# A diffusion backbone step: a warm-up, an earlier first product, moved query slices and later weight chunks in the first head

## What is computed

```python
c      = silu(c_ctx), silu(c)                    # two conditioning vectors of 2048
mod    = c @ w_ada + b_ada                       # w_ada 2048 x 6144: shift, scale, gate
h      = rms_norm(x, norm_w) * (1 + scale) + shift
proj   = h @ w_in                                # w_in 2048 x 9216, nine parts of 1024
# parts 0, 1: q, k of retention; 2, 3: its v and gate; 4, 5, 6: q and two forget
# gates of HGRN2; 7, 8: its v and gate; eight heads of 128 in each part
# two scans over chunks, forward and backward, per head and group
out    = concat(o_r, o_h) @ w_out                # 2048 x 2048
y      = rms_norm(x + gate * out) * final_norm_w
```

## Time and profile before

| | |
|---|---|
| median of 3 runs | 1426.14 us (1426.08 to 1426.21) |
| profiled execution | 1426.52 us, span 1424.7 us |
| TensorE busy | 1404.5 us, 99% of the span |
| TensorE loading weights | 1184.8 us, 83% |
| VectorE busy | 970.9 us, 68% |
| ScalarE busy | 496.7 us, 35% |
| GpSimd busy | 367.9 us, 26% |
| HBM read and written | 174.41 and 16.53 MB, 134 GB/s over the span |
| mean granted TensorE clock | 0.998 |

### The profile page before, as it was taken

One profiled execution on the slowest core, in us unless ns is written; L12 is line 12 of the kernel. 1 busy time (PEld: TensorE's weight loads), 2 busy tenths in 40 slices (PEclk: granted clock), 3 DMA queues, 4 the chain that ended last, 5 costly groups with the idle time before them and its releaser, 6 DMA issues.

```text
span 1424.7 us, 24851 instructions
## 1 busy us (share of the span) xinstructions
PE 1404.5 (99%) x10220; PEld 1184.8 (83%) x10220; DVE 970.9 (68%) x1293; ACT 496.7 (35%) x893; POOL 367.9 (26%) x292
## 2 busy tenths in 40 slices
PE   6999999999999999999999999999999999999997
PEld 4788898889888988898889888988898888888886
DVE  4655676666689778977887788766676668632345
ACT  4323243334333433343334333423342334321234
POOL 0000114311432153215321532153114315301220
PEclk9999999999999999999999999999999999999999
DMA  9994222322333333323432333322223347183235
GB/s 387 409 404 169 79 94 83 89 91 73 127 126 109 107 126 124 119 99 126 130 115 97 126 134 111 97 97 88 83 68 97 89 148 256 48 286 112 89 104 206
DMA packets 68870, 196.66 MB, mean 138 GB/s; under 512 B 7824, under 2 KB 16288, under 8 KB 63904
## 3 DMA queue, kind: packets, MB, share of 16 engines
q1 hardware_dynamic: 68736, 195.15, 39.7%
q10 hardware_dynamic: 32, 0.02, 0.0%
HBM read 174.41 MB, written 16.53 MB: 134 GB/s over the span
## 4 chain that ended last, share of the span: by engine, by line
PE 97%; DVE 1%; DMA 1%; ACT 0%; issue 0%; SPq 0%; DVEq 0%; ACTq 0%
PE ps L2013 10%; PE ps L2015 10%; PE ps L2014 10%; PE ps L1846 9%; PE ps L1848 8%; PE ps L1847 8%; PE ps L1822 8%; PE ps L2196 5%; PE ps L2198 5%; PE ps L2197 5%; PE ps L2030 2%; PE ps L1855 2%; PE ps L1853 2%; PE ps L1854 2%; PE ps L1812 2%; PE ps L2041 1%
## 5 line engine op out<-in xcount | busy, mean ns | idle before, releaser
L1139 DVE TENSOR_TENSOR w_lo<-area,w_hi 128x1024 fp32r<-128x1024 f32 x143 | 184.4, 1289 | 253.5 <-ACT w_hi L675 253.5
L675 ACT ACTIVATE w_hi<-area 128x1024 fp32r<-128x1024 f32 x143 | 151.7, 1061 | 500.4 <-PE ps L2015 292.8
L2013 PE MATMUL ps<-w_hi,hT_hi 128*128 128x512 f32 x640 | 252.1, 394 | 0.0
L2015 PE MATMUL ps<-w_hi,hT_lo 128*128 128x512 f32 x640 | 249.4, 390 | 0.0
L2014 PE MATMUL ps<-w_lo,hT_hi 128*128 128x512 f32 x640 | 249.2, 389 | 0.0
L1846 PE MATMUL ps<-hT_hi,w_hi 128*128 128x512 f32 x512 | 205.6, 401 | 0.5 <-DVE hT_lo L1191 0.4
L1847 PE MATMUL ps<-hT_lo,w_hi 128*128 128x512 f32 x512 | 199.7, 390 | 0.0
L1848 PE MATMUL ps<-hT_hi,w_lo 128*128 128x512 f32 x512 | 199.7, 390 | 0.0
L2015 PEld LDWEIGHTS ps<-w_hi,hT_lo 128*128 128x128 f32 x640 | 120.1, 188 | 25.4
L2013 PEld LDWEIGHTS ps<-w_hi,hT_hi 128*128 128x128 f32 x640 | 120.2, 188 | 24.3
L2014 PEld LDWEIGHTS ps<-w_lo,hT_hi 128*128 128x128 f32 x640 | 120.3, 188 | 24.0
(11 more groups left out here) (279 smaller groups left out, 2463.7 us busy)
## 6 DMA issues: line engine op xcount, KB each, us to landing
area<-in_w_in SPq DMA_DIRECT2D x144, 512.0 KB, 3.9
area<-in_w_mod SPq DMA_DIRECT2D x32, 1024.0 KB, 8.8
area<-in_w_out SPq DMA_DIRECT2D x38, 512.0 KB, 3.7
gate_raw<-in_w_gate SPq DMA_DIRECT2D x32, 512.0 KB, 3.7
o_hi_scratch<-area SPq DMA_DIRECT2D x14, 320.0 KB, 2.2
o_lo_scratch<-area SPq DMA_DIRECT2D x14, 320.0 KB, 2.9
hT_hi<-o_hi_scratch SPq DMA_DIRECT2D x14, 320.0 KB, 7.3
hT_lo<-o_lo_scratch SPq DMA_DIRECT2D x14, 320.0 KB, 8.1
```

The costliest lines, as they stand in the source:

```text
L675: act.activation(split_weights(h, n)[0], raw[:, n % 3, :], ACT.Copy).then_inc(wt_hi.sem, 1)
L1139: v.tensor_tensor(lo, raw[:, n % 3, :], hi.bitcast(F32), ALU.subtract).then_inc(wt_lo.sem, 1)
L2013: mm(out, hT_hi[:, k, tile_cols(t)], w_hi[:, n % 2, w], start=k == 0, stop=False)
L2015: i = mm(out, hT_lo[:, k, tile_cols(t)], w_hi[:, n % 2, w], start=False, stop=k == KT - 1)
```

## The change

It has six parts.

1. **Warm-up.** TensorE no longer starts with four matmuls of ones when the constants have landed, but with 11 matmuls of zeros as soon as VectorE has cleared `cs` (`cs_zero`), and then two of ones. VectorE writes `cs` after those 11 (`pe_warm`).
2. **Squares.** Squares 14 and 15 are added to each other and summed by TensorE as a group of their own; square 13 goes from TensorE to VectorE. TensorE still sums eight groups.
3. **First modulation.** Row 0 is copied by ScalarE, not by VectorE between two steps of `rstd`. Odd ones of the first four pieces use PSUM bank `C + 1`, and such a piece's chunks wait only for the piece two before it.
4. **First input slice.** ScalarE and VectorE do latents before context (`CLASSES`). For slice 0, VectorE subtracts latents and context apart (`first_low_input`), and the four latent products wait for the latents alone. Three idle matmuls after c2 are gone.
5. **Query slices** of w2 stand elsewhere in TensorE's order: from behind c11 on, one before each wait for columns.
6. **Loads.** w3 to w7 are requested behind the fourth chunk of their piece (c11, c15, c19, c23, c27), before behind the third. w2 goes from behind c8 to behind c7.

```diff
-WARM = 4
-PE_SQUARES = (1, 3, 5, 7, 9, 11, 13)
-DVE_SQUARES = (0, 2, 4, 6, 8, 10, 12, 14, 15)
+WARM = 11
+PE_SQUARES = (1, 3, 5, 7, 9, 11)
+DVE_SQUARES = (0, 2, 4, 6, 8, 10, 12, 13)
+LAST_SQUARES = (14, 15)
+SUMS = len(PE_SQUARES) + 2
...
         def ada_bank(piece):
-            return C
+            return C + piece % 2 if piece < SINGLES else C
...
-        CLASSES = ((0, slice(0, P)), (1, slice(P, T)))
+        CLASSES = ((1, slice(P, T)), (0, slice(0, P)))
...
-            chunks = {5: 1, 8: 2, 10: 3, 14: 4, 18: 5, 22: 6, 26: 7, 29: 8}
+            chunks = {5: 1, 7: 2, 11: 3, 15: 4, 19: 5, 23: 6, 27: 7, 29: 8}
...
             act.activation(rstd, rstd, ACT.Exp, scale=-0.5).then_inc(rstd_act.sem, 1)
+            act.wait_ge(a_used.sem, a_used.at(1))
+            act.activation(mod_row, ps[:, ada_bank(0), 0:ADA_TILE], ACT.Copy).then_inc(row_out.sem, 1)
...
+            dve.wait_ge(pe_warm.sem, pe_warm.at(0))
             for w in range(2):
                 i = v.tensor_copy(cs[:, :, w:w + 1], c_sig[:, w, :].unsqueeze(2))
...
+            pair = [x_squares[:, k % SQUARES, :] for k in LAST_SQUARES]
+            dve.wait_ge(x_sq.sem, x_sq.at(LAST_SQUARES[1]))
+            v.tensor_tensor(pair[0], pair[0], pair[1], ALU.add).then_inc(x_sum.sem, 1)
...
+            def first_low_input():
+                dve.wait_ge(latent_hi.sem, latent_hi.at(0))
+                dve.wait_ge(h_mod.sem, h_mod.at(0))
+                latents, context = slice(P, T), slice(0, P)
+                v.tensor_tensor(hT_lo[:, 0, latents], modulated[0][:, latents], hT_hi[:, 0, latents].bitcast(F32),
+                                ALU.subtract).then_inc(latent_lo.sem, 1)
+                dve.wait_ge(h_hi.sem, h_hi.at(0))
+                v.tensor_tensor(hT_lo[:, 0, context], modulated[0][:, context], hT_hi[:, 0, context].bitcast(F32),
+                                ALU.subtract).then_inc(h_lo.sem, 1)
...
             modulated_input(0)
+            first_low_input()
             normed_input(1)
-            low_input(0)
...
-                if piece >= 1 and first == 0:
-                    pe.wait_ge(mod_steps.sem, mod_steps.at(0, mods_known(piece - 1)))
+                before = piece - 2 if piece < SINGLES else piece - 1
+                if before >= 0 and first == 0:
+                    pe.wait_ge(mod_steps.sem, mod_steps.at(0, mods_known(before)))
...
             ada_chunk(2)
-            idle(3)
             first_group(0, 0, range(0, 2))
...
             ada_chunk(9)
+            first_group(1, 1, range(0, 3))
             ada_chunk(10)
-            first_group(1, 1, range(0, 3))
+            first_group(1, 1, range(3, 5))
+            first_queries(0, range(0, 1))
             ada_chunk(11)
-            first_group(1, 1, range(3, 4))
+            first_queries(0, range(1, 2))
             modulation_columns(4)
-            first_group(1, 1, range(4, 5))
+            first_queries(0, range(2, 3))
             ada_chunk(12)
-            first_queries(0, range(0, 1))
+            first_queries(0, range(3, 4))
             first_group(2, 0)
             ada_chunk(13)
-            first_queries(0, range(1, 3))
...
-                first_queries(0, range(e, e + 1 if e < WCHUNKS - 2 else KC))
+                first_queries(0, range(e + 1, e + 2))
```

## The result

The changed kernel takes 1429.28 us in the median of 14 runs (1428.15 to 1431.54), the kernel before 1426.18 us (1425.95 to 1426.33). The ratio is 1.0022, with a 95% interval from 1.0015 to 1.0028: 3.1 us slower, just over the 0.2% that the prediction took as the bound. It lies at the upper edge of the range. The forecast was 1427.2 us and no measurable change; the outcome is its second rival, slower by the closing loop, to which it gave 15%. The changed kernel also scatters: 3.4 us between its fastest and slowest run, against 0.4 us of the kernel before beside it (1.2 to 2.8 us in the 28 to 33 runs beside the experiments).

The account below looks back on a forecast made before the run. TensorE bounds the kernel, with full DMA queues limiting the front. 1.9 us won, less 0.5, 1.1, 0.7 and 0.7, ends the front 1.1 us later: 1427.2 us median, range 1424.6 to 1429.3.

Parts of the forecast that it names:

- second rival: Loop of request, landing, weight chunk and row: two pairs take 18.5 us plus the landing, against 24.0; 1429.8 us, 15%.
- What bounds the kernel: Whole run: TensorE holds 97% of the span; full DMA queue limits the front; nothing past 120 us matters.
- The sum: 1.9 us won, 0.5 lost to a chunk landing, 1.1, 0.7 and 0.7 at rows 4 to 6: front ends 1.1 later.
- The first 30 us: Start of the front: first product at 27.95 instead of 29.82 us, a lead of 1.9 us.
- The squares: Start of the front: ScalarE's 0.8 us loss to TensorE's sums goes, one addition less saves 0.3; reciprocal root starts 1.1 earlier.
- let it run at full speed by then: TensorE's first sums of squares: eleven matmuls of zeros from 1.3 us on end its slow stretch, so 0.8 us go.
- c5's limit: Modulation chunk c5 still lands at 34.6 us, its matmuls end at 35.7; the lead shrinks from 1.9 to 1.4 us.
- The late weight chunk: Weight chunks w3 to w7 land 2.53 us later, holding VectorE's row copy; TensorE waits 1.1, 0.7, 0.7 at rows 4 to 6.
- Rows 7 and 8 come to no wait by the same sum: Later front: w6 and w7, 2.53 us later, still reach their columns within TensorE's 12.0 us per pair; no cost.
- The Trainium skill's 2.0 us of fixed cost: Landing of c17 before row 6: 4.5 us instead of 5.4, total loss 0.6 instead of 1.1; the prediction didn't use it.
- The query slices: TensorE's order in the front: they only change places, 8 of 8 done by its end, so cost nothing in sum.
- The first rival: VectorE isn't held by the weight chunk, only c5's landing limits the lead: 1.4 us faster, 1424.7 us; 20%.

## Why the prediction was right and wrong

**What bounds the kernel**: right. Nothing past 120 us played a part, and the front has two limits, TensorE and the landings. The sum's lead agrees with the profile's to 0.3 us up to row 6.

**The first 30 us**: right in sum, partly for another reason. The first product came at 27.99 (27.95 was said):

```profile
26.98 1.08 PE L1832 MATMUL ps<-area 128*32 128x128 f32 x32 [1.75 <-DMA area<-in_w_mod]
27.99 0.50 PE L1866 MATMUL ps<-hT_hi,w_hi 128*128 128x512 f32 x1
...
33.33 2.21 PE L1832 MATMUL ps<-area 128*32 128x128 f32 x64
```

But two paths met there: VectorE had the low half of the latents at 27.79, and TensorE itself stood for 1.75 us before c2, which landed 19.9 us after its request, at 27.0, where the kernel before had it after 18.7, and was through with it at 27.99. The sum had only the first path. The squares won 0.95 us (ScalarE took the sum at 20.66, before at 21.61), but the landings of c2 and c5 gave none of it on, and the kernel without the warm-up is no slower. Nor did the matmuls of zeros "let it run at full speed by then": after waits of 1.24 and 0.64 us the first sum of squares took as long as before, and the granted clock fell:

```profile
8.35 2.07 PE L1918 MATMUL ps<-con 128*128 128x512 f32 x2 [0.64 <-ACT con L665]
...
12.22 1.02 PE L1918 MATMUL ps<-con 128*128 128x512 f32 x2
...
9.00:11.00 2.00, 2.00 (x5) 1.10 (x4) 0.97 (x2) 1.34 (x3) 0.00 (x0) 0.50 0.99 416
```

ScalarE still waited 0.3 us for sums, where the prediction had nothing left of the 0.8. c5's limit was right: its matmuls ended at 33.33 + 2.21 = 35.5, against 35.7 in the sum.

**The late weight chunk**: right in mechanism, and to 0.4 us in size. Rows 4, 5 and 6 were put at 57.5, 68.85 and 81.5 and came at 57.32, 68.54 and 81.75. The waits were 1.48, 0.83 and 0.98 us, for 1.1, 0.7 and 0.7 in the sum; at row 4 TensorE came at 55.84 and not at 56.4, since the moved work also takes away the 0.4 us for which the kernel before waits for c11 (at 53.34). That the row copy is what carries them is shown by the kernel that copies it first. c17 was requested at 65.14 (65.5 in the sum) and landed 5.8 us later, the upper of the two values taken as bounds for row 6 and not the 5.4 between them. The request and its time to landing, for c17 and then for c26:

```profile
65.14 0.33 SPq L452 DMA_DIRECT2D area<-in_w_mod  x1
...
area<-in_w_mod SPq DMA_DIRECT2D x1, 1024.0 KB, 5.8
...
92.27 0.33 SPq L452 DMA_DIRECT2D area<-in_w_mod  x1
...
area<-in_w_mod SPq DMA_DIRECT2D x1, 1024.0 KB, 6.7
```

**The step that failed** is the sentence "Rows 7 and 8 come to no wait by the same sum", and in that sum the landing after a late request, put at 5.4 us. Row 7 did come to no wait; row 8 waited 0.91 us. The second pair of rows above is c26, requested at 92.27, behind the wait of row 6, and landed 6.7 us later; w7 landed 10.4 us after c26's request, where the sum has 5.4 + 2.53 + 1.27 = 9.2. The prediction had the condition in its second rival, a loop that loses from a landing of 5.5 us on, and took a tenth less, where the shortest landing of a modulation chunk in the trace was 5.8. By its formula two pairs take 18.5 + 5.4 = 23.9 us, just under TensorE's 24.0; from row 6 at 81.75 to row 8 at 106.90 they took 25.15.

With 5.8 at row 6 the lead there would have been -1.5, and with 6.7 at row 8 -2.6 (81.95 + 10.4 + 6.7 + 8.07 = 107.1, against 104.5 at equal work), 1428.7 us for the median. The 0.6 us from there to the measured 1429.28 is the step from a profiled execution to the median: the sum takes 0.38 off, as in the kernel before, but the changed kernel's profiled execution lies 0.24 below its median. Putting w7 back or using c13 early each takes a turn out of this loop, for 1.5 and 1.4 us; w5 alone put back wasn't tried.

What the row hangs on is the weight chunk behind c17, c18 and c19, and c17's own landing doesn't tell when that comes. In the changed kernel with fillers c17 was requested at 65.15, here too with c16 alone in flight, and landed after 5.0 us instead of 5.8; ScalarE took w5 at the same time, 77.52 against 77.57:

```profile
area<-in_w_mod SPq DMA_DIRECT2D x1, 1024.0 KB, 5.0
...
77.52 1.06 ACT L678 ACTIVATE w_hi<-area 128x1024 fp32r<-128x1024 f32 x1 [5.46 <-DMA area<-in_w_in]
```

From c17's request to w5's landing it was 12.2 to 12.7 us in all six profiles with a late c17 and c18, c19 and w5 behind it, against 5.4 + 5.06 + 1.27 = 11.7 in the sum. So the late request costs the whole group 3.3 to 3.8 us beside its bytes (8.9 us at 414 GB/s), whichever part of that c17 shows. Why, no run shows.

**The Trainium skill's 2.0 us of fixed cost** ("DMA: Bandwidth & Descriptors", on the anatomy of one transfer) would have c17 land after 4.5 us; the page gives the figure for transfers issued by GpSimd, and SyncE issues these. For c17 by itself that is off by 1.3 us in the changed kernel, but by 0.2 to 0.6 in six other profiles, where it was requested between 64.2 and 65.4 us and landed after 4.7 to 5.1. For w5 it would be off by 1.6 us, and w5 counts. The prediction's sum with 4.5 has a slip as well: with columns at 80.65 and TensorE there at 80.85 row 6 costs nothing, and the front ends 0.4 us later, not 0.6.

**The second rival** (the loop closes) was the right mechanism. Its 1429.8 charged rows 6, 7 and 8, but by its own figures row 7, which hangs on row 5, is hidden behind the wait of row 6 (93.75 against 94.5), and without it the rival gives 1429.0.

**The query slices** "cost nothing in sum": true of work and wrong as a reason to leave them out. Without their move and that of the products of pair 1 the 1.4 us of the front are lost in front of c10 and c11 (1426.52 us, as fast as the kernel before). The list of the change ahead of the prediction names only the slices, "from behind c11 on"; the diff has the first of them before c11. The prediction saw that TensorE had waited for c11 before, and named it under a rival instead of in the sum.

**The first rival** (the lead survives) is out with these loads and is just what the old loads give: 1424.84 for its 1424.7.

**The clock**, given 3%, was there, if not where it was put. In the changed kernel's profile it fell at 8 us, among the first squares, and not again in the front. In two other profiles it fell behind waits of 1.75 and 2.58 us. How much of the scatter of the changed kernel is the clock and how much the landings, stays open: fillers at one of its waits took 1.0 us off the median, within its interval, and left one run above 1430.

## What to carry to other kernels

An in-order engine passes a late load on to everything that stands behind its wait, also to work that doesn't need the load; before a request is moved back, read which copy, and which engine behind that copy, stands behind its consumer. Where a buffer is asked for again only when it has been used, add up the whole turn (use, request, landing of what stands behind it, consumer, next use) and compare it with the work that a turn gives the busiest engine: here a turn took 25.15 us against 24.0 us of work, and a delay that looks paid once was paid again at the next turn. And where the DMA queue is full, an earlier engine only arrives earlier at the next landing, so a lead needs work without a load to stand before each landing; here the products of pair 1 and query slices of 1 us did that together, and made 1.4 us of a front that alone gave nothing.

## What the runs showed of the hardware

- The granted clock fell to 0.50 (1.2 of 2.4 GHz) behind a wait of 2.58 us, and in one of seven profiles behind a wait of 1.4 to 1.75 us for c2 (that one 1.75). In two profiles it fell at 8 us, behind waits of 1.24 and 0.64 us, and of 1.55 and 0.27 us. Each fall lasted 3 to 4 us. Behind the other waits in these profiles it stayed at 1.00. Behind the wait of 2.58 us its fall cost 1.3 us where it happened and 0.6 us at the end, since later landings took back the rest.
- The record of the granted clock doesn't show every slow stretch: in the kernel before it reads 1.00 from 7 to 10 us, where four filler matmuls took 2.07 us, and later the same four took 1.16. What slowed them, no row tells.
- c2's landing moved 1.2 us back when TensorE used c0 earlier. The request of c4, which waits for that use, went out at 21.70 instead of 22.65, while c3 and c2 were in flight. In all ten profiles with c4 requested by 21.78 us c2 landed 19.4 to 20.0 us after its own request, in the four with 22.06 or later after 18.1 to 18.7; c3's landing hardly moved (29.43 and 29.60). That c4's packets took some of c2's time is the likely cause, but wasn't tried apart.
- A chunk of 1 MB that was requested with one other load in flight landed after 4.7 to 6.8 us (15 times in ten profiles), against 2.53 us for its bytes at 414 GB/s. The same chunk, c17, requested within 0.2 us of the same time, landed after 4.7, 5.0, 5.1 and 5.8 us in four profiles.
